# The first mixer's attention with turns two pairs behind the scores and values three

## The reference, cut to what matters

```
# sparse: 8 heads, one key head, top 128 keys by an index score
score = einsum('bqh,bqhs->bqs', iw, relu(einsum('bqhe,bse->bqhs', iq, ik)))
_, sel = top_k(where(mask, score, -inf), 128)
prob = softmax(einsum('bqhd,bqkd->bhqk', q, k[sel]) * 64 ** -0.5)
a_out = einsum('bqhl,hld->bqhd', einsum('bhqk,bqkl->bqhl', prob, v_lat[sel]), w_uv)
# differential: 4 heads with two maps each
prob = softmax(where(mask, einsum('bqhcd,bshcd->cbhqs', q, k) * 64 ** -0.5, -inf))
b_out = rms_norm(einsum('bhqs,bshe->bqhe', prob[0] - lam * prob[1], v), g) * 0.8
mix = concat(a_out, b_out) @ w_out
```

## Time and profile before

| | us |
|---|---|
| median of 3 runs | 3141.97 |
| lowest and highest | 3140.49 and 3142.46 |
| the profiled execution's own time | 3145.03 |
| its span in the trace | 3143.4 |
| first scores of the stage to first matmul of the next | 520.76 to 670.76 |
| mean granted clock of TensorE | 0.989 |

### The profile page before, as it was taken

How to read it: one execution, slowest core, us unless ns; L and a number is a source line. 1 busy time by engine, 2 the same in 40 slices (tenths; PEclk the granted TensorE clock), 3 DMA queues, 4 the chain that set the end, 5 groups by cost and what they waited for, 6 DMA issues and landing times.

```text
span 3143.4 us, 36178 instructions
## 1 busy us (share of the span) xinstructions
PE 3042.2 (97%) x14292; PEld 2469.6 (79%) x14292; DVE 1296.9 (41%) x2360; ACT 1190.8 (38%) x2090; POOL 1106.5 (35%) x465
## 2 busy tenths in 40 slices
PE   8999998899999999999989999999999999999998
PEld 6888777678888878888758888877768878877787
DVE  5311286824121361111894231164735152257532
ACT  3322365643232342223424232245333252256522
POOL 4444432014444444444104444443424433310143
PEclk9999999999999999999999999999999999999999
DMA  4333232013333233333213333323313334410132
GB/s 148 94 94 101 88 116 79 1 34 101 100 94 96 92 94 96 99 95 99 91 47 107 94 100 95 96 92 115 101 54 94 94 108 155 137 35 2 34 95 74
DMA packets 78187, 278.27 MB, mean 89 GB/s; under 512 B 8599, under 2 KB 9495, under 8 KB 77636
## 3 DMA queue, kind: packets, MB, share of 16 engines
q1 hardware_dynamic: 78020, 275.96, 28.1%
HBM read 273.78 MB, written 6.08 MB: 89 GB/s over the span
## 4 chain that ended last, share of the span: by engine, by line
PE 86%; DVE 9%; ACT 2%; issue 1%; POOL 0%; DMA 0%; ACTq 0%; SPq 0%; DVEq 0%; POOLq 0%
PE ps L486 25%; PE ps L488 25%; PE ps L487 25%; PE ps L1571 2%; PE ps L1545 2%; DVE arena L2443 1%; PE ps L1557 1%; DVE arena L1827 1%; PE ps L3146 1%; PE ps L2493 1%; PE ps L1991 1%; DVE w_lo L471 1%; PE ps L2942 1%; PE ps L1977 1%; DVE arena L1910 0%
## 5 line engine op out<-in xcount | busy, mean ns | idle before, releaser
L461 POOL TENSOR_TENSOR w_lo<-ring,w_hi 128x1024 fp32r<-128x1024 f32 x449 | 1092.0, 2434 | 1905.3 <-ACT w_hi L438 1905.3
L486 PE MATMUL ps<-x_hi,w_hi 128*128 128x512 f32 x2168 | 857.7, 396 | 28.7 <-DVE x_lo L872 13.1
L488 PE MATMUL ps<-x_hi,w_lo 128*128 128x512 f32 x2168 | 847.4, 391 | 0.0
L487 PE MATMUL ps<-x_lo,w_hi 128*128 128x512 f32 x2168 | 847.2, 391 | 0.0
L438 ACT CAST w_hi<-ring 128x1024 fp32r<-128x1024 f32 x473 | 493.9, 1046 | 727.8 <-PE ps L488 720.6
L486 PEld LDWEIGHTS ps<-x_hi,w_hi 128*128 128x128 f32 x2168 | 409.3, 189 | 121.0 <-issue 21.7
L487 PEld LDWEIGHTS ps<-x_lo,w_hi 128*128 128x128 f32 x2168 | 409.5, 189 | 88.3 <-issue 4.1
L488 PEld LDWEIGHTS ps<-x_hi,w_lo 128*128 128x128 f32 x2168 | 409.1, 189 | 85.8
L486 PE MATMUL ps<-r_hi,w_hi 128*128 128x512 f32 x1120 | 436.4, 390 | 0.0
L487 PE MATMUL ps<-r_lo,w_hi 128*128 128x512 f32 x1120 | 435.9, 389 | 0.0
L488 PE MATMUL ps<-r_hi,w_lo 128*128 128x512 f32 x1120 | 435.8, 389 | 0.0
(11 more groups left out here) (269 smaller groups left out, 3305.8 us busy)
## 6 DMA issues: line engine op xcount, KB each, us to landing
ring<-in_stream SPq DMA_DIRECT2D x473, 512.0 KB, 3.5
arena<-in_cmp_w SPq DMA_DIRECT2D x16, 512.0 KB, 3.8
frev_copies<-frev SPq DMA_DIRECT2D x16, 240.0 KB
arena<-frev_copies SPq DMA_DIRECT2D x1, 3072.0 KB, 13.0
h<-in_x SPq DMA_DIRECT2D x4, 512.0 KB, 7.6
out<-arena SPq DMA_DIRECT2D x4, 512.0 KB
arena<-in_p SPq DMA_DIRECT2D x2, 512.0 KB
arena<-in_mem SPq DMA_DIRECT2D x1, 1024.0 KB
```

Of the source, the lines that this page charges most:

```text
L461: self.nc.gpsimd.tensor_tensor(self.w_lo[:, n % SPLIT, :], self.ring[:, n % RING, :], self.w_hi[:, n % SPLIT, :].bitcast(F32), ALU.subtrac ...
L486: nc.tensor.matmul(out, a[0], b[0], start=start, stop=False)
L487: nc.tensor.matmul(out, a[0], b[1], start=False, stop=False)
L488: return nc.tensor.matmul(out, a[1], b[0], start=False, stop=stop)
```

## The change

Each pair's turn is made two rounds behind its scores and its values three, one round later than before on every engine. ScalarE's round is reordered: store of `it - 4`, copy of `it - 2`, factors of `it - 1`, exponentials of `it`. What is counted from the depth moves with it: SubNorm begins in round 24, where it was 23, Lift's rounds are 15, 32, 33 and 36, where they were 14, 31, 32 and 35, and there are 37 rounds instead of 36. The roundings for the next stage stay in round 32. No buffer is added.

```diff
-    norm_at = joined + 3
+    norm_at = joined + 4
@@
-        free = max(free + 1, last[i] + 4)
+        free = max(free + 1, last[i] + 5)
@@
-    turns = max(max(lift_at), norm_at + 7, n + 3) + 1
+    turns = max(max(lift_at), norm_at + 7, n + 4) + 1
@@ TensorE
                 if it < n:
                     scores(it)
-                if 1 <= it < n + 1:
-                    turn(it - 1)
                 if 2 <= it < n + 2:
-                    values(it - 2)
+                    turn(it - 2)
+                if 3 <= it < n + 3:
+                    values(it - 3)
@@ VectorE
-                if 3 <= it < n + 3 and pairs[it - 3].joined:
-                    store(it - 3)
+                if 4 <= it < n + 4 and pairs[it - 4].joined:
+                    store(it - 4)
@@ ScalarE
-                if 3 <= it < n + 3 and not pairs[it - 3].joined:
-                    store(it - 3)
+                if 4 <= it < n + 4 and not pairs[it - 4].joined:
+                    store(it - 4)
+                if 2 <= it < n + 2:
+                    copy(it - 2)
+                if 1 <= it < n + 1:
+                    scale(it - 1)
                 if it < n:
                     exponentials(it)
-                if 1 <= it < n + 1:
-                    copy(it - 1)
-                if it < n:
-                    scale(it)
```

## The result

The changed kernel took 3174.22 us (median of 4 runs, 3173.88 to 3176.16) against 3142.22 us (4 runs, 3140.49 to 3142.49) before: a ratio of 1.0103, with a 95% interval of 1.0092 to 1.0115, or +32.0 us. The prediction was 3162, with a range that ended at 3174. The direction was right, the size was not: the sum said +20.0.

What follows compares the result with a forecast made beforehand. VectorE bounds rounds 0 to 23; TensorE is nearly full from 640.9 us. Terms: 14.8 - 5.0 - 1.1 + 0 + 7.5 + 3.8 = +20.0 us, so 3165.0 on the profiled scale, 3162.0 as median; range 3147 to 3174.

Steps and rivals of the forecast that it cites:

- old waits: Rounds 0 to 23: VectorE's waits for scores go as the distance to ScalarE's factors grows to three rounds; -5.0 us.
- slower still: the clock: Rival: longer waits drop six more groups of 16 matmuls to half speed; +10 us, 3172.0; chance 0.14.
- New waits of rounds 5 to 22, 14.8: VectorE's reciprocal waits for exponentials in rounds 5, 8, 11, 13, 16, 18, 20 and 22; 14.8 us, bounds 8 to 19.
- Squares, -1.1: SubNorm's squares, one round later, directly follow the exponentials instead of copy and factors; -1.1 us, bounds -2 to 0.
- Rounds 24 to 27, 0: New waits for exponentials against one SubNorm product fewer ahead of the scores of 28; 0 us, bounds -2 to +4.
- Rounds 28 to 30, +7.5: Loop from scores to next scores: exponentials now wait for turn, copy and factors; +7.5 us, bounds +3 to +9.
- Tail, +3.8: Behind the last scores: one more turn and one more values of four tiles left on TensorE; +3.8 us.
- TensorE and ScalarE run ahead: Rival, rounds 3 to 23: turn and copy finish before VectorE's bias, so no new waits; -6.2 us, 3135.8; chance 0.06.
- V(r-4): TensorE's values of pair r-4: need the store of r-5, issued at VectorE's round r-1 start, which forbids any lead.
- The rule weighed against the trace: TensorE's waits for ScalarE's factors: keep the matmul engine busy, so removing them gains all; -19.2 us.
- No change: Rival: exponentials wait only in rounds of 384 columns, 6.6, plus 3.8 at the end, against 9.96 gained; 3142.4 us; chance 0.10.

Runs made afterwards that it cites:

- short fillers: The changed kernel plus 103 matmuls with unused results in TensorE's waits, half as many as in a run before: 3164.57 us, ratio 1.0070.
- the copy last: The changed kernel with ScalarE's round reordered to factors of p-1, exponentials of p, then copy of p-2: 3143.32 us, ratio 1.0002.

## Why the prediction was right in kind and short in size

**The mechanism held.** The chain was to run from VectorE's store over values, scores, turn, copy and factors to the exponentials. The timeline of round 5 shows it in that order, its end was cut off by moving the exponentials (-29 and -31 us), and its beginning by moving the store (the first stretch back at 86.6 us). At the old depth the order alone brings +23.7.

**The step that failed is the place given to the clock.** (A second, smaller one is the -5.0 for old waits, below.) The prediction's sum took every link at 2.4 GHz (the turn of four tiles 2.05, scores 0.92) and put "slower still: the clock" beside it as a rival with a chance of 0.14 and +10 us. It was no alternative: the forecast's own waits are what lets the clock fall, so if the forecast holds the rival holds too, and belongs in the sum. The runs show both: with the clock better kept (0.95, 0.84 and 1.00 by stretches) the change costs +22.2 against the kernel before on the same chip (3164.57 - 3142.40; 23.2 by the stretches of its profile), the chain's own price; the change as it is costs 9.6 more. 20 and 10 were both close, and added they make 3172, the time that the prediction gave to the clock rival. It had them as two cases, and so took 3162. That its +10 came out so near is in part luck: it supposed six turns at the lower clock, and in the profiles the difference lies in the first stretch (3.2), between biases 25 and 28 (1.8), in the products and scores of the loop (3.7) and in the tail (1.1), with 0.6 lost at the squares.

**The terms one by one**, measured first in the change and then with short fillers:

- *New waits of rounds 5 to 22, 14.8.* The reciprocals of rounds 5, 7, 8, 11, 13, 14, 16, 18, 20 and 22 waited 3.40, 1.95, 0.68, 4.18, 1.42, 0.59, 2.28, 1.27, 0.97 and 0.75 us, together 17.5. With fillers it was 2.33, 0.60, 3.36, 2.70, 1.42, 0.59, 2.29, 1.01, 0.96 and 0.75, together 16.0. Eight of the ten rounds were named, 13, 18, 20 and 22 with values within 0.3 (1.5, and 1.0 each). Round 5's 2.2 was right at full clock (2.33) and a third short without it. Rounds 7 and 14 weren't foreseen (round 7 waited 0.60 before the change too). Round 8's 2.2 was 0.68 in the change, behind the long wait of round 7, and 3.36 with fillers. Round 16's 3.7 was too much: 2.28, and 1.05 of a bias that waited for scores. From bias 0 to bias 23 all the reciprocal's waits together grew from 3.35 us to 19.58, so by 16.2, and to 18.09 with fillers, by 14.7. The term was right once the clock was kept.
- *Old waits, -5.0.* This is the second term that failed. In the same stretch VectorE's other waits with a named releaser (for scores, values or itself) were 3.2 us before, 2.9 in the change and 1.3 with fillers. So 0.3 to 1.9 us went, not 5.0. Of the 5.25 us that the prediction added up, 2.02 were waits of reciprocals for exponentials, which a longer distance to the factors does not remove: with the copy last the reciprocal still waited 3.2 us up to bias 23. The first stretch as a whole came to +15.1 for a predicted +9.8, and to +11.9 with fillers. Of the miss 3.2 are the clock, and the other 2.1 lie in this term (with fillers 1.9 of named waits and 1.0 of gaps and work came back, 2.9 in all).
- *Squares, -1.1.* -0.8 measured, but this stretch depends on the clock of SubNorm's small products, which took 4.24 us in the change, 5.14 before and 3.70 to 6.96 over the runs.
- *Rounds 24 to 27, 0.* +2.1. The bounds of -2 to +4 took it in. With fillers it was +0.4, although the store behind L2173 is there as well; so most of it hung on the slow matmuls.
- *Rounds 28 to 30, +7.5.* +11.1, and +7.4 with fillers. The bounds ended at +9. Here the mechanism and the arithmetic stand (2.0 us more from bias to exponentials, for the predicted 2.3), and what was mis-sized is the product and the scores behind the wait, at 2.05 and 1.74 us for 1.10 and 1.13. A smaller slip: the old third loop took 4.82 us, not 5.44 as the two others.
- *Tail, +3.8.* +4.8, because the first turn behind the last scores took 3.11 us. At full speed it is +3.7 (17.8 against 14.1).

**The signs.** The bias was to wait for scores hardly at all before 600 us, and it did: one wait, of 1.05 us, at 598.66. The time from bias 28 to bias 29 was to be 7.6 us and was 8.98 (7.42 with fillers). The turn behind the last scores was to begin 18 us before the next stage; it began at 683.65, 19.0 before. The reciprocal's waits were put at 20 to 28 us and were 41.7. That figure did not even follow from the prediction's own terms: 9.2 of before, 14.8 and 7.5 make 31.5, and the 1.4 to 1.9 us that it names for each of rounds 24 to 27 come on top. Adding up one's own terms for each sign would have caught it.

**Rivals.** "TensorE and ScalarE run ahead" fell as argued, by V(r-4) tied to the store; the waits it would have removed did go (19.2 to 3.9 us), and the kernel lost 32 us. The rule weighed against the trace, to keep the matmul engine busy (the Trainium skill, Perfetto Trace Analysis, Optimization Strategies), would have made the change 19 us faster. The waits it looks at were slack, as the earlier trace rows said. "No change" needed a free loop in rounds 28 to 30, which cost 11.1 us. "Slower still: the clock", with its chance of 0.14, came nearest: 3172.0 for 3174.22. A second rule of the Trainium skill (Perfetto Trace Analysis, Matmul Optimizations) says that the matmul engine scales its power with its utilization, so that matmuls should go back to back in batches; the trace agrees, with a granted clock of 0.88 in the change's first stretch and 0.95 once its waits were partly filled.

**What stays open.** The fillers raise the clock and take TensorE's time at once, so 9.6 us is what they gave back net, and the clock's full price may be more (the second stretch was still at 0.84). Why the clock fell further in one execution of the same instructions than in another (134.9 and 140.6 us up to bias 28) is open. The stretches are each read from one profile of a kernel, so differences of 1 to 3 us between them are uncertain; the medians of the whole program are not.

## What to carry to other kernels

In a round of a software pipeline, an engine's queue should begin with what the bounding engine waits for. An operation that needs something another engine makes *in the same round* belongs at the round's end, however old the pair it serves: one pair of lines in the wrong order cost 24 to 31 us here, and the depth by itself almost nothing. A pipeline stage more isn't free at the end of the loop either; count what it leaves behind the last round (3.7 us).

And if a forecast adds long waits to TensorE (here of 2.5 to 4.3 us), the slower matmuls behind them are a term of the sum and not another scenario: here 9.6 us on top of 22. An old wait may be booked as a gain only if the change removes what it waits for.

## What was not expected of the hardware

- Matmuls whose results nobody uses made two kernels faster: 103 of them took the change from 3174.22 to 3164.57 us, and 43 took the copy-last kernel from 3143.32 to 3136.91 (5.9 us, each against its own runs of the kernel before). The granted clock of the first stretch rose from 0.88 to 0.95 and from 0.88 to 0.94.
- Their number matters as much as their place: twice as many gave a higher clock (0.98) and no time (3172.89 us).
- One such matmul of 128 by 128 in float32 shows as two records and takes 0.23 us at full clock (3.74 us for 16).
- SubNorm's 16 one-column matmuls (L2184, 32 records) do almost no arithmetic, and yet the clock counts for them: 5.80 us without and 3.70 us with fillers ahead of them, and between 4.24 and 6.96 us in two executions whose instructions up to there are the same.
